# A decoder trunk step on one core: smaller first loads, the state product at the close of its tile, samples stored in pairs of halves

## What is computed

```
h = rms_norm(x, norm1);  z = h @ w_in            # 2048 x 5120: u, q, f, i, g of 1024 each
u: four groups of 256 channels, trailing means of 2, 4, 8, 16 tokens minus the token, @ w_pool, * scale
   (15 cached rows go ahead of each sample sequence; the last 15 rows are an output)
8 heads of 128: forget = lb + (1 - lb) * sigmoid(f);  S_t = diag(forget_t) S_(t-1) + (1 - forget_t)^T i_t
   o_t = silu(q_t) S_t;  o = o * rsqrt(mean(o*o) + eps) * hg_norm * silu(g);  the last S is an output
x = x + concat(pool, o) @ w_o
x = x + (silu(h2 @ w_gate) * (h2 @ w_up)) @ w_down    # h2 = rms_norm(x, norm2), inner width 5632
y = rms_norm(x, norm_f)
```

## Time and profile before

| | |
|---|---|
| median of three runs | 1423.66 us |
| the profiled execution | 1423.26 us |
| its span | 1421.5 us |
| TensorE busy | 1400.6 us, 99% of the span |
| VectorE, ScalarE, GpSimd busy | 777.9, 569.5, 220.7 us |
| moved by DMA | 214.5 MB |

### The profile page before, as it was taken

One profiled execution on the slowest core, in us unless ns is written; L12 is line 12 of the kernel. 1 busy time (PEld: TensorE's weight loads), 2 busy tenths in 40 slices (PEclk: granted clock), 3 DMA queues, 4 the chain that ended last, 5 costly groups with the idle time before them and its releaser, 6 DMA issues.

```text
span 1421.5 us, 28076 instructions
## 1 busy us (share of the span) xinstructions
PE 1400.6 (99%) x10256; PEld 1386.4 (98%) x10256; DVE 777.9 (55%) x1202; ACT 569.5 (40%) x924; POOL 220.7 (16%) x329
## 2 busy tenths in 40 slices
PE   8999999999999999999999999999999999999996
PEld 6999999999999999999999999999999999999996
DVE  5668888887755544444444444444444444444443
ACT  5545555555533333333333333333333333333343
POOL 0255555555322100000000000000000000000131
PEclk9999999999999999999999999999999999999998
DMA  8545565555555555545655555565554565554453
GB/s 237 167 135 156 161 168 160 149 149 153 161 148 148 148 148 148 148 130 145 172 146 148 148 138 143 148 166 158 143 157 119 151 175 153 149 148 138 123 142 115
DMA packets 408217, 214.50 MB, mean 151 GB/s; under 512 B 4205, under 2 KB 405821, under 8 KB 408124
## 3 DMA queue, kind: packets, MB, share of 16 engines
q1 hardware_dynamic: 388775, 202.01, 52.1%
q10 hardware_dynamic: 19413, 12.10, 2.9%
HBM read 206.20 MB, written 7.89 MB: 151 GB/s over the span
## 4 chain that ended last, share of the span: by engine, by line
PE 98%; DMA 1%; issue 0%; DVE 0%; ACTq 0%; DVEq 0%; ACT 0%
PE bank L416 31%; PE bank L418 30%; PE bank L417 30%; DMA xt<-in_x_sample 1%; PE bank L533 1%; PE bank L657 0%; PE bank L492 0%; PE bank L763 0%; PE bank L493 0%; PE bank L494 0%; PE bank L699 0%; PE bank L632 0%; PE bank L701 0%; PE bank L700 0%; PE bank L590 0%
## 5 line engine op out<-in xcount | busy, mean ns | idle before, releaser
L416 PE MATMUL bank<-a_hi,w_hi 128*128 128x320 f32 x2016 | 626.4, 311 | 2.8 <-issue 2.8
L418 PE MATMUL bank<-a_hi,w_lo 128*128 128x320 f32 x2016 | 623.0, 309 | 0.0
L417 PE MATMUL bank<-a_lo,w_hi 128*128 128x320 f32 x2016 | 622.8, 309 | 0.0
L1170 DVE TENSOR_TENSOR w_lo<-w_raw,w_hi 128x1024 fp32r<-128x1024 f32 (+1 forms) x412 | 459.0, 1154 | 133.9 <-ACT w_hi L807 132.6
L807 ACT ACTIVATE w_hi<-w_raw 128x1024 fp32r<-128x1024 f32 (+1 forms) x412 | 383.5, 968 | 159.4 <-PE bank L418 138.3
L416 PEld LDWEIGHTS bank<-a_hi,w_hi 128*128 128x128 f32 x2016 | 378.5, 188 | 4.2 <-issue 3.4
L417 PEld LDWEIGHTS bank<-a_lo,w_hi 128*128 128x128 f32 x2016 | 378.5, 188 | 0.7
L418 PEld LDWEIGHTS bank<-a_hi,w_lo 128*128 128x128 f32 x2016 | 378.4, 188 | 0.0
L416 PE MATMUL bank<-h_hi,w_hi 128*128 128x320 f32 x704 | 218.5, 310 | 0.0
L418 PE MATMUL bank<-h_hi,w_lo 128*128 128x320 f32 x704 | 217.4, 309 | 0.0
L417 PE MATMUL bank<-h_lo,w_hi 128*128 128x320 f32 x704 | 217.3, 309 | 0.0
(11 more groups left out here) (262 smaller groups left out, 1214.4 us busy)
## 6 DMA issues: line engine op xcount, KB each, us to landing
w_raw<-in_w_gate SPq DMA_DIRECT2D x44, 1024.0 KB, 5.6
w_raw<-in_w_up SPq DMA_DIRECT2D x44, 1024.0 KB, 5.6
w_raw<-in_w_down SPq DMA_DIRECT2D x64, 704.0 KB, 4.8
w_raw<-in_w_in SPq DMA_DIRECT2D x38, 1024.0 KB, 5.8
w_raw<-in_w_o SPq DMA_DIRECT2D x16, 1024.0 KB, 6.1
s<-in_state_hgrn ACTq DMA_DIRECT2D x8, 512.0 KB, 4.3
out<-sn ACTq DMA_DIRECT2D x8, 512.0 KB, 5.3
xt<-in_x_prompt SPq DMA_DIRECT2D x6, 256.0 KB, 9.0
```

What stands on the lines that cost most here:

```text
L416: pe.matmul(out, whi[:, par_, cols], r_hi, start=(k == 0), stop=False)
L417: pe.matmul(out, whi[:, par_, cols], r_lo, start=False, stop=False)
L418: last = pe.matmul(out, wlo[:, par_, cols], r_hi, start=False, stop=(k == last_k))
L1170: dve.tensor_tensor(wlo[:, par_, cols], raw[:, par_, cols], whi[:, par_, cols].bitcast(F32), SUB)\
```

## The change

The edits, in the order of the program:

- **First loads** in five chunks of 2, 2, 4, 4 and 4 tiles (`CHUNKS`). ScalarE's queue takes the prompt tile 1 and the sample tile of the first two chunks, SP's queue all the rest and all first weights. `keep_busy(4)` becomes `keep_busy(1)`; two transposes ahead at first, and the transposes of tile k + 3 stand behind the matmuls of tile k. VectorE copies the residual of tile 0 and of the odd tiles after the low part; the cast pieces stand behind tiles 1, 3, 7 and 11. The rms broadcast moves from tile 3 to tile 6.
- **Pooling states**: the tails hold the 8 new rows of each sample sequence and the 15 of the prompt, 79 rows, with one transpose for two and one copy for two. The 7 old rows of each sample sequence go from the cache to the output by one DRAM to DRAM copy on SP's queue, ahead of the heads' weights.
- **Heads**: the values' transposes stand behind the scores. The state product moves from the middle of the unit to its end, ahead of the outputs, and the product with `s1` becomes the last of the outputs, with `o_mm` on it. VectorE casts the first half of the next unit before the state copy and the second after it.
- **Newton** in three instructions for four.
- **Samples in pairs**: for the tiles 0 to 7 the scaled sample columns are written to columns 0 to 63 of a tile of `yt`, for 8 to 15 to columns 64 to 127 of the same tile, and one transpose turns both, so that partitions 0 to 63 hold the first 1024 columns of the 64 tokens and 64 to 127 the second. The sample piece is scaled and stored last, as 128 rows of 1024, to a destination of two halves by 64 tokens by 1024. The dummy matmuls ahead of the means go; the means are taken for both halves of the partitions; the early ones stand in the middle of the last unit.

```diff
+CHUNKS = ((0, 2), (2, 4), (4, 8), (8, 12), (12, 16))
+def sample_pair(j, half):
+    return yt[:, 2, bass.ds(HD + P * j - half * HD, P)]
+BEHIND = (1, 3, 7, 11)
+X_ACT = tuple(range(2, KD, 2))
+X_DVE = (0,) + tuple(range(1, KD, 2))
...
-Y_DVE = ((0, slice(0, 512)), (0, slice(512, 1024)), (2, slice(0, D)), (1, slice(0, 1024)))
+Y_DVE = ((0, slice(0, 512)), (0, slice(512, 1024)), (1, slice(0, 1024)), (2, slice(0, HD)))
 Y_ACT = ((0, slice(1024, D)), (1, slice(1024, D)))
...
-    for quarter in range(4):
-        load_x(sp, quarter, 0)
-        if quarter >= 2:
-            load_x(sp, quarter, 1)
-        if quarter != 1:
-            first_weights(sp, quarter)
+    for chunk in range(5):
+        load_x(sp, chunk, 0)
+        if chunk >= 2:
+            load_x(sp, chunk, 1)
+            load_x(sp, chunk, 2)
+        first_weights(sp, chunk)
     load_params(sp, PARAMS[1:], par_loaded)
-    sp.wait_ge(first_lo, 2)
+    sp.wait_ge(first_lo, 3)
     sp.dma_start(raw[:, 0, :].rearrange("p (k c) -> p k c", c=P), win_v[:, :, 2 * P:3 * P]).then_inc(w2_loaded, 16)
     sp.dma_start(cache_t[:, :], cache_pool[0].rearrange("b t c -> (b t) c")).then_inc(cache_loaded, 16)
-    sp.wait_ge(first_lo, 4)
+    sp.wait_ge(first_lo, 5)
     sp.dma_start(raw[:, 1, :].rearrange("p (k c) -> p k c", c=P), win_v[:, :, 3 * P:4 * P]).then_inc(w3_loaded, 16)
...
+    sp.dma_start(pool_sample[0, :, 0:CACHE - TS, :], cache_pool[0, :, TS:CACHE, :]).then_inc(out_done, 16)
     with sp.Fori(0, HEADS) as h:
...
+    by_halves = bass.AP(y_sample.tensor, y_sample.offset, [[HD, 2], [D, NS], [1, HD]])
     for i, (t, cols) in enumerate(Y_DVE):
-        dst = y_prompt[0, t * P:(t + 1) * P, cols] if t < 2 else y_sample.rearrange("b t d -> (b t) d")[:, cols]
+        dst = y_prompt[0, t * P:(t + 1) * P, cols] if t < 2 else by_halves
         sp.wait_ge(y_scaled_v, i + 1)
-        sp.dma_start(dst, yt[0:(P if t < 2 else NS), t, cols]).then_inc(out_done, 16)
+        sp.dma_start(dst, yt[:, t, cols]).then_inc(out_done, 16)
...
-            pe.wait_ge((xres_act, alo_ready)[k % 2], (k // 2 - 1, k - 3)[k % 2])
+            if k - 4 in X_DVE:
+                pe.wait_ge(xres_dve, X_DVE.index(k - 4) + 1)
+            else:
+                pe.wait_ge(xres_act, X_ACT.index(k - 4) + 1)
...
-    keep_busy(4)
+    keep_busy(1)
     pe.wait_ge(fill_done, 3)
     pe.wait_ge(x_pad, 1)
-    for k in range(AHEAD):
+    for k in range(2):
         x_transposes(k)
     for k in range(KD):
-        if k + AHEAD < KD:
-            x_transposes(k + AHEAD)
...
+        for ahead in ((2, 3) if k == 0 else (k + AHEAD,)):
+            if ahead < KD:
+                x_transposes(ahead)
...
         for c in range(2):
-            pe.transpose(TK[0:NB * CACHE, c * P:(c + 1) * P], tails[:, c, 0:NB * CACHE], ident)
-            last = pe.transpose(TK[0:CACHE, TP + c * P:TP + (c + 1) * P], tails[:, c, NB * CACHE:], ident)
+            last = pe.transpose(TK[0:NS + CACHE, c * P:(c + 1) * P], tails[:, c, :], ident)
...
     def spread_rms(k):
-        if k == 3:
+        if k == 6:
...
         sample_thrice(TK, k_rep).then_inc(k_tr, 1)
-        pe.wait_ge(unit_read, n)
-        pe.wait_ge(v_thrice, r + 1)
-        pe.transpose(TV[:, 0:P], vv[:, 0:P], ident)
-        pe.transpose(TV[:, P:TP], vv[:, P:TP], ident)
-        sample_thrice(TV, v_rep).then_inc(v_tr, 1)
         pe.wait_ge(mp_lo_s, HEADS)
...
         last.then_inc(sc_mm, 1)
+        pe.wait_ge(unit_read, n)
+        pe.wait_ge(v_thrice, r + 1)
+        pe.transpose(TV[:, 0:P], vv[:, 0:P], ident)
+        pe.transpose(TV[:, P:TP], vv[:, P:TP], ident)
+        sample_thrice(TV, v_rep).then_inc(v_tr, 1)
...
                 at = QSTEP * b - TS * i
-                last = pe.matmul(out[j * HS:(j + 1) * HS, :], qm[:, at:at + HS], s0[:, b, :], start=False,
-                                 stop=(i == 1))
-        last.then_inc(o_mm, 1)
...
     def rec_out(r):
         after(pe, gated, r)
-        pe.wait_ge(s1_ready, r + 1)
         pe.wait_ge(sc_put, PUTS * (r + 1))
         pe.matmul(OT[:, 0:P], sc[:, 0, :], vt[:, 0, :], start=True, stop=True)
-        pe.matmul(OT[:, P:TP], sc[:, 1, :], vt[:, 1, :], start=True, stop=False)
-        pe.matmul(OT[:, P:TP], qr[LP][:, CH:TP], s1[:, :], start=False, stop=True)
         pe.matmul(OT[:, TP:TP + P], scs[:, :], vt[:, 2, :], start=True, stop=False)
         rec_s0(r)
         pe.wait_ge(vm_ready, r + 1)
...
             last = pe.matmul(bk[:, :].rearrange("p (b v) -> p b v", v=P), k3[:, i, :], vm[:, i, :, :],
                              start=True, stop=True)
         last.then_inc(sn_mm, 1)
+        pe.matmul(OT[:, P:TP], sc[:, 1, :], vt[:, 1, :], start=True, stop=False)
+        pe.wait_ge(s1_ready, r + 1)
+        pe.matmul(OT[:, P:TP], qr[LP][:, CH:TP], s1[:, :], start=False, stop=True).then_inc(o_mm, 1)
...
-        unit(n, par_, a_rhs, between=(lambda: rec_state(r), lambda: rec_out(r)))
+        def go():
+            rec_state(r)
+            rec_out(r)
+        unit(n, par_, a_rhs, between=(None, go))
...
     part_of(0, 0, 8, used=1)
+    part_of(0, 8, own)
     rec_state(HEADS - 1)
-    part_of(0, 8, own)
     rec_out(HEADS - 1)
...
-                for i, (t0, t1) in enumerate(((0, P), (P, TP), (TP, N))):
-                    last = pe.transpose(bk[0:t1 - t0, i * P:(i + 1) * P], x2g[:, par_, t0:t1], ident)
+                for i in range(2):
+                    last = pe.transpose(bk[:, i * P:(i + 1) * P], x2g[:, par_, i * P:(i + 1) * P], ident)
+                if half:
+                    last = pe.transpose(bk[:, TP:TP + P], sample_pair(j, 1), ident)
                 last.then_inc(y_tr, 1)
...
             def column_means(out_bank, src, signal):
-                for i, (t0, t1) in enumerate(((0, P), (P, TP), (TP, N))):
-                    last = pe.matmul(out_bank[0:t1 - t0, i:i + 1], src[:, t0:t1], meanc[:, 0:1],
-                                     start=True, stop=True)
+                for i in range(2):
+                    pe.matmul(out_bank[:, i:i + 1], src[:, i * P:(i + 1) * P], meanc[:, 0:1], start=True, stop=True)
+                for rows in (slice(0, NS), slice(NS, P)):
+                    last = pe.matmul(out_bank[rows, 2:3], src[:, TP:N], meanc[:, 0:1], start=True, stop=True)
                 last.then_inc(signal, 1)
-            pe.wait_ge(x2_acc, KD - 1)
-            for bk in (TV, OT):
-                pe.matmul(bk[:, 2:3], acc[:, N - P:N], meanc[:, 0:1], start=True, stop=True)
-            column_means(TV, acc, y_early)
+            def early_means():
+                pe.wait_ge(x2_acc, KD - 1)
+                column_means(TV, acc, y_early)
+            unit(nd + KD - 2, 0, h_rhs, HALF_D, between=(None, y_tiles(KD - 3, 1, 1)))
+            unit(nd + KD - 1, 1, h_rhs, HALF_D, between=(early_means, y_tiles(KD - 2, 0, 1)))
             pe.wait_ge(last_sq, 1)
             column_means(OT, sq, stat_mm)
-            y_tiles(KD - 1, 1)()
+            y_tiles(KD - 1, 1, 1)()
...
-    for quarter in range(4):
-        if quarter < 2:
-            load_x(act, quarter, 1)
-        if quarter == 1:
-            first_weights(act, 1)
-        load_x(act, quarter, 2)
+    for chunk in range(2):
+        load_x(act, chunk, 1)
+        load_x(act, chunk, 2)
...
-        if k % 2 == 0:
+        if k in X_ACT:
             act.activation(x1[:, k, :], bk[:, 0:N], ACT.Copy).then_inc(xres_act, 1)
-        if k % 4 == 1 and k < 12:
-            first_piece(k // 4 + 1)
+        if k in BEHIND:
+            first_piece(BEHIND.index(k) + 1)
         if k == 8:
             square(0, 0)
-        if k == 11:
-            square(0, 1)
         if k == 13:
             act.wait_ge(w2_loaded, 16)
             hi_piece(2, 0, 0, HALF[0])
+    square(0, 1)
+    hi_piece(2, 0, 1, HALF[1])
     square(0, 2)
     square(1, 0)
-    hi_piece(2, 0, 1, HALF[1])
     act.wait_ge(w3_loaded, 16)
     hi_piece(3, 1, 0, HALF[0])
...
-    act.dma_start(pool_sample[0].rearrange("b t c -> (b t) c"), st_s[:, :]).then_inc(out_done, 16)
-    act.dma_start(pool_prompt[0, 0], st_p[:, :]).then_inc(out_done, 16)
+    act.dma_start(pool_sample[0, :, CACHE - TS:CACHE, :], st_new[0:NS, :]).then_inc(out_done, 16)
+    act.dma_start(pool_prompt[0, 0], st_new[NS:NS + CACHE, :]).then_inc(out_done, 16)
...
-            act.activation(x2g[:, par_, :], x2[:, par_, :], ACT.Copy, scale=pcol("norm_f", j))\
-               .then_inc(x2_scaled, 1)
-        def y_copy(j, par_):
+            act.activation(x2g[:, par_, :], x2[:, par_, 0:TP], ACT.Copy, scale=pcol("norm_f", j))
+            act.activation(sample_pair(j, half)[:, half * NS:(half + 1) * NS], x2[:, par_, TP:N], ACT.Copy,
+                           scale=pcol("norm_f", j)).then_inc(x2_scaled, 1)
...
-            act.activation(yt[0:NS, 2, bass.ds(j * P, P)], bk[0:NS, TP:TP + P], ACT.Copy).then_inc(y_copied, 1)
+            last = act.activation(yt[:, 0:2, bass.ds(j * P, P)], bk[:, 0:TP].rearrange("p (c v) -> p c v", c=2),
+                                  ACT.Copy)
```

(67 more changed lines are left out.)

120 lines of the change are left out of this document (62 added, 58 removed).

## The result

The changed kernel takes 1424.33 us, median of 20 runs (1423.19 to 1427.08); the kernel before beside it on the same chip 1422.96 (1420.55 to 1424.05). The ratio is 1.0014, 95% interval 1.0008 to 1.0021: slower by a little, within the 0.2% that the prediction counts as no change, and 2.6 us above the 1421.7 forecast. All parts but one came out as gains; the store gave them back and a bit more. The profiled execution is the slowest of its twenty, 1427.08 (span 1425.3), so its rows at the start show a worse case than the median.

A forecast was written before the change was run, and what follows sets the result against it. The prediction took TensorE, busy 99% of the span, as the bound. Its terms, -6.0 - 0.9 - 2.3 - 0.9 + 0.9 + 7.6 = -1.6 against 1423.26, gave 1421.7 us, range 1412 to 1425.3.

The forecast's parts named there:

- step 6: Final stores: the sample store with outermost count 2 is served by only two engines, +7.6 us.
- 26 each: Final stores: 16 engines when full move 414 GB/s, 26 GB/s for each engine.
- Rival A: Final stores: they spread over all engines, 1412.8 us; chance 0.20.
- step 1: Start: five first chunks for four quarters end the first stage at 29.2, -6.0 us (bounds -7.3 and -2.9).
- I take 1.3 us for that and the clock: Start: 1.3 us allowed for the second chunk landing late and the half clock.
- Rival B: Start: half clock as long as now and chunk 2 late, -2.9 for -6.0, 1424.8 us; chance 0.08.
- step 3: Head turns: value transposes behind the scores shrink the gap to 0.15, -2.3 us (bounds 0 and -3.1); state product 0.
- rival C: Heads: waits for s1 take the place of the slack, +5.6 us, 1427.3 us; chance 0.07.
- steps 2, 4, 5: Pool states, fewer transposes, -0.9 us; paired samples, fewer transposes, -0.9; means and scales at the end, +0.9.

The follow-up runs named there:

- e1: Changed kernel with its one sample store cut into two stores of 64 rows each: 1415.54 us, ratio 0.9953.
- e6: Kernel before, its sample store described on the memory side with an outermost count of 2 that can't be joined: 1432.43 us, ratio 1.0074.
- e8: Kernel before with the changed kernel's start alone (five chunks, queues, transposes behind the matmuls, `keep_busy(1)`): 1417.38 us, ratio 0.9966.
- experiment 8: Why the full kernel's start is later: e12 with the down loop unrolled, 1414.87 us; changed kernel with `x2g` at its old size, 1424.26 us.
- e3: Changed kernel with ScalarE's wait for the third unit's weights moved from behind tile 13 to behind tile 15: 1423.69 us, ratio 1.0010.
- e7: Changed kernel with the sample store in two of 64 rows and ScalarE's wait for the third unit's weights behind tile 15: 1414.67 us, ratio 0.9944.
- g2: e12 with the last block's down loop unrolled as in the changed kernel: 1414.87 us, ratio 0.9949.
- e4: Changed kernel with the value transposes of a head back ahead of its scores: 1426.93 us, ratio 1.0033.
- e5: Changed kernel with each head's state product back in the middle of the tile: 1424.91 us, ratio 1.0018.
- e9: Kernel before with the changed order in the heads alone: 1420.23 us, ratio 0.9986.
- e12: Kernel before with new start, heads, pool states and Newton loop, ScalarE's weights wait behind tile 15; samples, down loop, stores as they were: 1414.25 us, ratio 0.9941.
- e10: Kernel before with paired samples, earlier means and the changed scales, sample store in two of 64 rows: 1421.35 us, ratio 0.9989.

## Why the prediction was right or wrong

**The store (step 6) was right in mechanism and short in size.** The forecast took +7.6; e1 gives +8.8 and the two profiles 19.22 - 10.49 = +8.7. The rate "26 each" holds where one queue is alone on the two engines, 53 GB/s together from 1417 on. What it missed is the stretch before, in which they also had ScalarE's pieces: 37 GB/s for the 3 us from 1414, an estimated 0.9 us lost (3 x 16 / 53). The samples went nearly all after the other stores, from 1412.8 to 1424.5, whereas the sum let both loads share the time from the first byte. Rival A (all engines, 1412.8) is refuted by e6 and e1 together. What it would have been worth is e1's 1415.5.

**The start (step 1) is where the forecast failed most: -6.0, of which the full kernel got about -4.5.** That is worked out: the median of the changed kernel, 1424.33, less 1.8 around the span, 19.2 and 1372.8, leaves 30.5 for the stage end, and 1422.96 of before less 1.8, 10.5 and 1375.7 leaves 35.0; the six profiles with the old start show 33.6 to 35.3. The failing term is "I take 1.3 us for that and the clock". First matmul: 8.18, better than the 9.2 forecast. Then TensorE stood 1.4 us for the third chunk's x, 1.4 for its weights and 2.0 at tile 14, 4.8 us in the profile for the 1.3. The step had the third chunk ready at "about 14 us"; its weights landed at 13.6 and their low part was done at 15.96. The last wait is one that the step didn't follow: the third unit's weights are issued only when the third chunk's are cast, they take 10 to 12 us to land, and ScalarE waits for them in the middle of the loop with two high parts queued behind. Alone the new start gave -5.0 (e8), within the bounds of -7.3 and -2.9. What the full kernel lacks against that goes with both things of experiment 8, the later third chunk and the longer stall: the same working gives stage ends of 29.9, 29.5 and 29.7 for e3, e7 and g2, where the wait is moved, and 30.8 to 31.3 for e1, e4 and e5, where it is not. How much of it the unrolled loop brings, which no step of the prediction had, is not settled. Rival B (half clock as long as before, -2.9) describes a part of the profiled execution: the clock did fall to 0.50, but at 32 us, behind that stall, not at the first chunk.

**Heads (step 3): right.** -2.3 forecast, -2.2 measured (e9), +2.6 when undone (e4). The turn measured in e9 is 0.31 us shorter, the 0.3 that the forecast took by letting each gap shrink to 0.15. The state product is neutral (e5) and no s1 wait shows, so rival C (1427.3) didn't happen.

**Pool states, samples, end (steps 2, 4, 5): -0.9 forecast in sum.** The second stretch shows it best: 1375.75 before, 1373.33 with the heads alone (e9), 1372.48 in e12, which adds the pool states and the Newton step (and the new start, outside this stretch): -0.85 for the -1.1 forecast (-0.9 and -0.2), and in it a new wait of 0.3 for `vm` that no step had. Samples and end together are read from e7 against g2, both unrolled and both with 0.8 of that wait: 1372.70 - 1372.91 = -0.2; e10 gives -0.2 to -0.35. The forecast had 0 (-0.9 + 0.9), so they are a small gain. e7 against e12 shows +0.2 only because e12 waits 0.5 less for `vm`. The early means took 0.64 in the last unit for 0.94 forecast. What the step hadn't seen is that the second set waits 0.8 us for the squares in any case.

**Sum.** Forecast -6.0 - 3.2 + 7.6 = -1.6. Measured, by the stretches: 30.5 - 35.0 = -4.5, 1372.8 - 1375.7 = -2.9, +8.7: +1.3, as the medians have it (1424.33 - 1422.96 = +1.4). Of the 3.0 between them the start has 1.5, the store 1.1, the rest 0.3. The time lies inside the range, 1412 to 1425.3, and within 0.2% of before, but on its slower side: the forecast said a little faster, and the kernel is a little slower by a margin clear of its interval. Two errors of the same sign, the start's and the store's, turned it.

## What to carry to other kernels

Before a transfer is reshaped to save work elsewhere, look at its outermost count on both sides after joining: where the end of the kernel waits for it, a count of 2 cost 8.7 us here, more than all the other parts of the change brought together (7.4). Two stores of 64 rows instead of one of 2 x 64 cost an issue and nothing else. When loads are moved to one queue, follow each load to what waits for it, and everything that stands in order behind that wait. And where a loop ends in many tiny matmuls, work of 0.4 us queued behind them closes the gap at the turn. When the profiled executions of two kernels are compared, look first where each lies among the times of its kernel: one from the slow end against one from the fast end shows a difference that the medians don't.

## What the hardware showed that was not expected

- With one queue on it, one DMA engine needs 159 ns for a 4 KB piece of a store and 88 ns for a 2 KB one. With pieces of two queues the same engines moved a tenth to a third less at the same share of their time: 37 GB/s for 53, 44 for 50, 73 for 98.
- The gap of 0.4 to 0.6 us at the turn of TensorE's loop depends on what was issued last: present in 7 of 7 turns behind the tiny score matmuls (before, e4), in none behind four transposes (e9). The turn gets 0.31 us shorter, not 0.46.
- An unrolled loop that runs at 1350 us went with a longer DMA issue on SP at 5 us (2.20 for 1.02) and, in the profiled executions, with a third chunk landing later (9.7 us for 7.6) and a later first stage. The cause is open.
- Executions of one kernel differ by up to 3.9 us, and the profiled one may be the slowest.
